# Square sums on VectorE, roots per group on all partitions, rotary keys copied ahead in one hybrid SSD/attention layer

## The chip, the cores and the metric

One core of a Trainium2 chip runs the whole layer. The metric is the device time in microseconds of one execution, from a launch of the program to its end; the median of three runs stands for a kernel. One execution was also recorded by the hardware profiler; its span is the stretch from the first recorded instruction to the last.

## What is computed

One layer of a streaming encoder for 256 prompt frames and 32 sample frames, which share the weights (T = 288 columns), in fp32:

```python
proj = x @ lp['w_in']
gate_pre, z, xbc, dt_raw, q_a, kv_a = jnp.split(proj, IN_SPLITS, axis=-1)
xbc, conv_new = _causal_conv(xbc, conv_state, lp['conv_w'], lp['conv_b'])
...
yh, s_fin = _ssd(xh, dt, a, bm, cm, s0, chunk)
yh = yh + xh * lp['d_skip'].reshape(SSM_GROUPS, HEADS_PER_GROUP, 1)
yg = (yh.reshape(bsz, L, D_INNER) * jax.nn.silu(z)).reshape(bsz, L, SSM_GROUPS, D_INNER // SSM_GROUPS)
yg = _rmsnorm(yg).reshape(bsz, L, D_INNER) * lp['ssm_norm_g']
y_ssm = yg @ lp['w_ssm_proj']
q = ((_rmsnorm(q_a) * lp['q_norm_g']) @ lp['w_q_b']).reshape(bsz, L, MLA_HEADS, QK_NOPE + QK_ROPE)
...
ckv = _rmsnorm(ckv) * lp['kv_norm_g']
kpe = _rope(kpe[:, :, None, :], pos)[:, :, 0, :]
...
mix = (g_ssm * y_ssm + g_mla * y_mla) @ lp['w_out']
h = _layernorm(ALPHA * x + mix, lp['ln1_g'], lp['ln1_b'])
ff = jnp.square(jax.nn.relu(h @ lp['w_up'])) @ lp['w_down']
y = _layernorm(ALPHA * h + ff, lp['ln2_g'], lp['ln2_b'])
```

Three places matter here. `_rmsnorm` is taken over the 512 features of each of two latents (`q_a` and `kv_a`), and over the 256 features of each of the 8 SSD groups. The rotary key `kpe` is 64 features wide.

## The kernel before

Features lie on the 128 partitions and the 288 frames on the free axis, so each activation is a row of blocks of 128x288. A weight chunk is 128x1024 in fp32 (512 KB). SyncE loads the chunks in the order of `chunk_order` into a ring of five slots. For each chunk ScalarE writes a rounded copy `whi` (`hi`, line 908) and VectorE the rest `wlo` (`lo`, line 1300); `ahead(name)` does this for the chunk three places behind the one named. TensorE multiplies in three passes (high by high, high by low, low by high) with operands of type fp32r, in `dense`: 24 matmuls of 288 columns a chunk. Semaphores order the work; every engine runs its own list in the order written.

The stages, in the order of the chunks:

- q0 to q3 and c0 to c3, the two latents. ScalarE squares each block into `qksq` (`latent`), `lat_sums(j)` adds four squared blocks over partitions and blocks by four matmuls with a matrix of ones, ScalarE takes the root, VectorE the reciprocal and the product (`lat_norm`). These ones-matmuls take plain fp32 operands.
- x0 to x31, the conv blocks, the first four ahead of attention and the others among the four attention rounds. `conv_in(b)` on ScalarE takes the block out of PSUM and starts the conv; for that GpSimd has copied three columns of history into `xp` (line 1873, semaphore `xp_state`), and later copies the new history out (line 1875, `xp_saved`). In GpSimd's list conv(0) comes first, then eight copies of the rotated key `krot` onto four quarters of the partitions (`kab`, `kall`, lines 1882 to 1888), four DMAs for the cached keys, and then conv(1).
- The SSD stage, groups 0 to 7. In each, TensorE runs z (two chunks), the gates gs and gm, `outputs`, `states`, and from group 1 on the attention projection m of the group before in two chunks, with small matmuls between: `tokens(g,0..2)`, `cb_products`, `decay_rows(g+1)`. VectorE makes the decay logarithms (`decay_log`), ScalarE their exponentials (`decays`), VectorE `products`, `tokens`, `gated`, `end_state`. `tokens(g,t)` on TensorE writes the bank that VectorE's `tokens` empties (`btok`, line 1546). In group 1 VectorE also splits the attention output (`o_low`, line 1614) for m. `square_sums(g)` adds the squares of two blocks by two ones-matmuls (lines 762 and 763).
- The norm of the groups: `variance` on ScalarE copies a 32-partition slice of the sum into `rstd`; four groups fill the 128 partitions. `roots(h)` then takes one root and `norm_rows(h)` one reciprocal for four groups. `spread(j, bank)` (line 755) puts a group's row back on all partitions by a matmul with a column of the identity. So groups 0 to 3 are normed in iterations 4 to 7 and groups 4 to 7 behind the loop, where `normed`, `norm_high` and `norm_low` write the two parts of `yn`.
- s (the SSD projection, reads `yn`), o, u (32 chunks), d (32 chunks), and the last layernorm.

ScalarE works with function tables; where a new function is not in the loaded set, the list has an ACT_TABLE_LOAD before it.

Of the kernel before, what the change touches and what calls it, by code (L numbers as in the profile page):

```python
# [5 lines left out]
F32 = mybir.dt.float32  # L6
F32R = mybir.dt.float32r
ALU = mybir.AluOpType
# [138 lines left out]
def yn_slot(j):  # L147

    return XB + 4 * (j // 8) + j % 4 + 8 * ((j % 8) // 4)


def layer_program(nc, wst, xT, misc, vecs, consts, ukT, cacheT, cacheK, kpeT, stateS, stateC,
                  o_y, o_ckv, o_kpe, o_ssm, o_conv):
    ctx = ExitStack()
    with ctx:
# [169 lines left out]
        def sems(*names):  # L325
# [27 lines left out]
        s_done, s_ready, sq_done, ss_done, var_in, std_done, rstd_done, bc_done = sems(  # L353
            "s_done", "s_ready", "sq_done", "ss_done", "var_in", "std_done", "rstd_done", "bc_done")
        norm_t, norm_h, norm_lo = sems("norm_t", "norm_h", "norm_lo")
# [68 lines left out]
        def _(pe):  # L424
# [35 lines left out]
            def lat_sums(j):  # L460
                pe.wait_ge(lat_sq, RB * j + RB)
                for k in range(RB):
                    mm = pe.matmul(ps_att[j][:, 0:T], ones, qksq[:, RB * j + k, :], start=k == 0, stop=k == RB - 1)
                mm.then_inc(lat_sum, 1)
# [287 lines left out]
            def spread(j, bank):  # L752

                pe.wait_ge(rstd_done, j // 4 + 1)
                pe.matmul(bank[:, 0:T], ident[:, 32 * (j % 4):32 * (j % 4) + 1].to_broadcast([P, P]),
                          rstd[:, j // 4, :], start=True, stop=True).then_inc(bc_done, 1)

            def square_sums(g):
                pe.wait_ge(sq_done, g + 1)
                if g >= 4:  # L760
                    pe.wait_ge(norm_t, g - 3)
                pe.matmul(ps_ss[:, 0:T], ones, sqs[:, 0, :], start=True, stop=False)
                pe.matmul(ps_ss[:, 0:T], ones, sqs[:, 1, :], start=False, stop=True).then_inc(ss_done, 1)
# [8 lines left out]
            for g in range(GROUPS):  # L772
# [12 lines left out]
                if g >= 4:  # L785
                    pe.wait_ge(var_in, g)
                    spread(g - 4, ps_ss)
# [6 lines left out]
                if g:  # L794
                    dense(("m", g - 1, 1), out, o_rows, 8, False, True)
                    pe.wait_ge(var_in, g)
# [17 lines left out]
            for b in range(4):  # L814
                if b == 0:
                    pe.wait_ge(var_in, GROUPS)
                    pe.wait_ge(s_ready, GROUPS)
                    spread(4, ps_ss)
                    spread(5, ps_s)
                dense(("s", b, 0), ps_att[b], yn_rows, 0, True, False)  # L820
                if b == 1:
                    pe.wait_ge(norm_t, 5)
                    spread(6, ps_ss)
                    pe.wait_ge(norm_t, 6)
                    spread(7, ps_s)
# [1287 lines left out]
```

## Time and profile before

| | us |
|---|---|
| Median of three runs | 857.95 (857.86 to 858.18) |
| The profiled execution | 857.47 |
| Its span | 855.7 |
| TensorE matmul busy | 828.9 (97%) |
| VectorE busy | 568.5 (66%) |
| ScalarE busy | 471.3 (55%) |
| GpSimd busy | 79.7 (9%) |
| Conv blocks 0 to 3 and the way to attention | about 41 to 60 |
| SSD stage | about 336 to 557 |

In the profile PE is TensorE, DVE VectorE, ACT ScalarE and POOL GpSimd. A row of a timeline gives the start and the length of an instruction or of several merged ones (x8 is eight records), and in brackets how long its engine had been idle and what it waited for. Records of matmuls overlap, since they are pipelined: the share of the path that one takes is the step from one start to the next.

### The profile page before, as it was taken

To read this page: it belongs to the slowest core of one execution; us is meant where nothing else is said; L and a number is where in the kernel's file an instruction comes from. 1 tells how busy PE (TensorE), PEld (TensorE's weight loads), DVE (VectorE), ACT (ScalarE), POOL (GpSimd) and SP (SyncE) were. 2 spreads that over 40 slices of the span, in tenths; PEclk is the share of its full clock that TensorE was granted. 3 is DMA by queue.
4 is the path that set the end of the run, shared out by engine and by line. 5 is a ranking of instruction groups with operands and counts; after the bars stand their busy time and mean duration, and the time that the engine had idled before them with its cause. 6 is when DMAs were issued, how large, how long until landed. Compare 5 with 4: busy or idle time off the path is not lost.

```text
span 855.7 us, 15623 instructions
## 1 busy us (share of the span) xinstructions
PE 828.9 (97%) x6359; PEld 787.1 (92%) x6359; DVE 568.5 (66%) x947; ACT 471.3 (55%) x817; POOL 79.7 (9%) x144
## 2 busy tenths in 40 slices
PE   6989999999999999999999999999999999999994
PEld 5988999999899899889998999999999999999994
DVE  5676756655565664886759677676679788755554
ACT  5674546466565466655464455444456888733432
POOL 0053002011011011100000000000000000001112
PEclk9999999999999999999999999999999999999998
DMA  7457325326325423434444353455554545545531
GB/s 289 126 178 291 103 82 176 107 62 196 121 74 173 124 74 116 143 117 124 142 119 140 113 151 114 134 205 165 160 168 149 171 158 164 164 159 172 170 126 56
DMA packets 34183, 123.57 MB, mean 144 GB/s; under 512 B 4224, under 2 KB 4368, under 8 KB 33856
## 3 DMA queue, kind: packets, MB, share of 16 engines
q1 hardware_dynamic: 30816, 110.67, 40.1%
q0 software_dynamic: 3104, 11.24, 3.8%
q8 instruction: 51, 0.84, 0.4%
q10 hardware_dynamic: 192, 0.66, 0.2%
q14 instruction: 20, 0.16, 0.1%
HBM read 118.52 MB, written 4.04 MB: 143 GB/s over the span
## 4 chain that ended last, share of the span: by engine, by line
PE 83%; ACT 6%; DVE 6%; DMA 2%; issue 1%; POOL 1%; ACTq 0%; DVEq 0%; POOLq 0%
PE ps_acc L426 15%; PE ps_acc L428 14%; PE ps_acc L427 14%; PE ps_row L428 3%; PE ps_row L426 3%; PE ps_row L427 3%; PE ps_s L611 3%; PE ps_cb L428 2%; PE ps_tr L428 2%; PE ps_tr L426 2%; PE ps_cb L426 2%; PE ps_tr L427 2%; PE ps_cb L427 2%; ACT prob L1026 2%; DVE wlo L1300 1%; DMA wraw<-in_wst 1%
## 5 line engine op out<-in xcount | busy, mean ns | idle before, releaser
L1300 DVE TENSOR_TENSOR wlo<-wraw,whi 128x1024 fp32r<-128x1024 f32 x204 | 249.4, 1225 | 189.5 <-ACT whi L908 189.1
L908 ACT CAST whi<-wraw 128x1024 fp32r<-128x1024 f32 x204 | 213.2, 1046 | 127.4 <-DMA wraw<-in_wst 126.9
L426 PE MATMUL ps_acc<-xh,whi 128*128 128x288 f32 x576 | 178.2, 309 | 8.3 <-DVE wlo L1300 8.3
L428 PE MATMUL ps_acc<-xh,wlo 128*128 128x288 f32 x576 | 171.0, 297 | 0.0
L427 PE MATMUL ps_acc<-xl,whi 128*128 128x288 f32 x576 | 169.1, 294 | 0.0
L426 PEld LDWEIGHTS ps_acc<-xh,whi 128*128 128x128 f32 x576 | 109.0, 189 | 15.0 <-DVE wlo L1300 8.3
L427 PEld LDWEIGHTS ps_acc<-xl,whi 128*128 128x128 f32 x576 | 110.1, 191 | 0.6
L428 PEld LDWEIGHTS ps_acc<-xh,wlo 128*128 128x128 f32 x576 | 108.8, 189 | 0.0
L1349 DVE SCALAR_TENSOR_TENSOR cv<-xp,vec,cv 128x292 f32<-128x292 f32 x96 | 50.3, 524 | 9.1 <-ACT cv L973 6.7
L426 PE MATMUL ps_acc<-o_h,whi 128*128 128x288 f32 x128 | 39.9, 311 | 0.0
L1875 POOL COPY cnew<-xp 128x6 f32<-128x6 f32 x32 | 15.4, 480 | 241.8 <-ACT xp L970 241.8
L428 PE MATMUL ps_acc<-o_h,wlo 128*128 128x288 f32 x128 | 37.9, 296 | 0.0
L427 PE MATMUL ps_acc<-o_l,whi 128*128 128x288 f32 x128 | 37.4, 293 | 0.0
L426 PE MATMUL ps_acc<-q_h,whi 128*128 128x288 f32 x96 | 29.7, 310 | 3.8 <-ACT xp L970 2.4
L428 PE MATMUL ps_acc<-q_h,wlo 128*128 128x288 f32 x96 | 29.0, 302 | 0.0
L427 PE MATMUL ps_acc<-q_l,whi 128*128 128x288 f32 x96 | 28.6, 298 | 0.0
L428 PE MATMUL ps_row<-e_h,wlo 128*128 128x290 f32 x96 | 28.6, 298 | 0.0
L426 PE MATMUL ps_row<-e_h,whi 128*128 128x290 f32 x96 | 28.6, 297 | 0.0
L427 PE MATMUL ps_row<-e_l,whi 128*128 128x290 f32 x96 | 28.5, 297 | 0.0
L426 PEld LDWEIGHTS ps_acc<-o_h,whi 128*128 128x128 f32 x128 | 24.0, 188 | 1.8 <-issue 0.7
L969 ACT COPY xp<-ps_acc 128x32 f32<-128x32 f32 x32 | 5.9, 183 | 35.2 <-PE ps_acc L428 35.2
L427 PEld LDWEIGHTS ps_acc<-o_l,whi 128*128 128x128 f32 x128 | 24.3, 190 | 0.3
(431 smaller groups left out, 2245.5 us busy)
## 6 DMA issues: line engine op xcount, KB each, us to landing
wraw<-in_wst SPq DMA_DIRECT2D x204, 512.0 KB, 3.5
side<-in_ukT POOLq DMA_DIRECT2D x8, 256.0 KB, 3.8
side_v<-in_ukT POOLq DMA_DIRECT2D x8, 256.0 KB, 3.0
out_ssm<-s_out POOLq DMA_DIRECT2D x8, 256.0 KB, 2.5
x<-in_xT SPq DMA_DIRECT2D x2, 576.0 KB, 4.7
ax<-in_xT POOLq DMA_DIRECT2D x1, 1152.0 KB, 6.0
out_y<-d SPq DMA_DIRECT2D x4, 288.0 KB, 2.1
ckvT<-in_cacheT POOLq DMA_DIRECT2D x1, 1024.0 KB, 7.0
```

The lines of the kernel that those rows point to most:

```text
L426: pe.matmul(out, w, mh, start=first, stop=False)
L427: pe.matmul(out, w, ml, start=False, stop=False)
L428: return pe.matmul(out, wl, mh, start=False, stop=last)
L611: mm = pe.matmul(ps_s[:, c * P:(c + 1) * P], ckvK[0:n, j, c * P:(c + 1) * P], ssT[0:n, j, :], start=j == 0, stop=j == 4)
L908: act.copy(whi[:, s % RING, :], wraw[:, s % RING, :]).then_inc(split_hi, 1)
L969: act.copy(xp[:, u, 264:XW], acc_of(name)[:, SEQ:T])
L1026: e = act.activation(prob[:, h4, a:b], prob[:, h4, a:b], ACT.Exp, bias=stat[:, 1, 4 * q + h4:4 * q + h4 + 1], accum_out=stat[:, 2, 4 * q + ...
L1300: tt(wlo[:, s % RING, :], wraw[:, s % RING, :], whi[:, s % RING, :].bitcast(F32), ALU.subtract).then_inc(split_lo, 1)
L1349: stt(cv[:, u, :], xp[:, u, 1 + tap:1 + tap + CW], v1(V_CONVW + tap * CB + b), cv[:, u, :], ALU.mult, ALU.add).then_inc(tap_chain if tap < ...
L1875: pool.tensor_copy(cnew[:, b, :].rearrange("p (a c) -> p a c", a=2), xp[:, u, 8:XW].rearrange("p (a c) -> p a c", c=36)[:, 6:8, 33:36]).th ...
```

## The change

- `lat_sums(j)`: VectorE adds the four squared blocks in two steps (`lat_squares`, 128x576 and 128x288) and TensorE multiplies once. `lat_squares(0)` stands in VectorE's list after the first half of the rotated key, `lat_squares(1)` before conv(0).
- `square_sums(g)`: VectorE adds the two squared blocks (`square_add`, behind `end_state`) and TensorE multiplies once.
- `spread`, `variance`, `roots` and `norm_rows` go. `root(g)` takes the root of the whole sum on 128 partitions straight from PSUM, one per group, behind `decays(g+1)`; `inverse_root` takes one reciprocal per group. `rstd` keeps two groups. The group g-1 is normed in iteration g, and only the last one behind the loop.
- `yn_slot` puts the low parts of a group over that group's own B and C blocks.
- GpSimd copies the histories of conv blocks 0 and 1 first, then the rotary keys, issues the four DMAs, and then takes conv(0).

```diff
...
 
-    return XB + 4 * (j // 8) + j % 4 + 8 * ((j % 8) // 4)
+    return XB + j // 2 + GROUPS * (j % 2)
 
...
             "tr_done", "tr_free", "xdt_done", "wx_done", "sdec_done", "y_done", "y_free", "yz_done")
-        s_done, s_ready, sq_done, ss_done, var_in, std_done, rstd_done, bc_done = sems(
-            "s_done", "s_ready", "sq_done", "ss_done", "var_in", "std_done", "rstd_done", "bc_done")
-        norm_t, norm_h, norm_lo = sems("norm_t", "norm_h", "norm_lo")
+        s_done, s_ready, sq_done, ss_done, std_done, rstd_done = sems(
+            "s_done", "s_ready", "sq_done", "ss_done", "std_done", "rstd_done")
+        norm_t, norm_h, norm_lo, sq_sum, lat_add = sems("norm_t", "norm_h", "norm_lo", "sq_sum", "lat_add")
         mix_g, mix_t, mix_hi, mix_lo, ax_in, ax_done = sems(
...
             def lat_sums(j):
-                pe.wait_ge(lat_sq, RB * j + RB)
-                for k in range(RB):
-                    mm = pe.matmul(ps_att[j][:, 0:T], ones, qksq[:, RB * j + k, :], start=k == 0, stop=k == RB - 1)
-                mm.then_inc(lat_sum, 1)
+                pe.wait_ge(lat_add, 2 * j + 2)
+                pe.matmul(ps_att[j][:, 0:T], ones, qksq[:, RB * j, :], start=True, stop=True).then_inc(lat_sum, 1)
 
...
 
-            def spread(j, bank):
-
-                pe.wait_ge(rstd_done, j // 4 + 1)
-                pe.matmul(bank[:, 0:T], ident[:, 32 * (j % 4):32 * (j % 4) + 1].to_broadcast([P, P]),
-                          rstd[:, j // 4, :], start=True, stop=True).then_inc(bc_done, 1)
-
             def square_sums(g):
-                pe.wait_ge(sq_done, g + 1)
-                if g >= 4:
-                    pe.wait_ge(norm_t, g - 3)
-                pe.matmul(ps_ss[:, 0:T], ones, sqs[:, 0, :], start=True, stop=False)
-                pe.matmul(ps_ss[:, 0:T], ones, sqs[:, 1, :], start=False, stop=True).then_inc(ss_done, 1)
+                pe.wait_ge(sq_sum, g + 1)
+                if g:
+                    pe.wait_ge(std_done, g)
+                pe.matmul(ps_ss[:, 0:T], ones, sqs[:, 0, :], start=True, stop=True).then_inc(ss_done, 1)
 
...
                 states(g)
-                if g >= 4:
-                    pe.wait_ge(var_in, g)
-                    spread(g - 4, ps_ss)
                 if g:
...
                     dense(("m", g - 1, 1), out, o_rows, 8, False, True)
-                    pe.wait_ge(var_in, g)
                     square_sums(g)
...
             for b in range(4):
-                if b == 0:
-                    pe.wait_ge(var_in, GROUPS)
-                    pe.wait_ge(s_ready, GROUPS)
-                    spread(4, ps_ss)
-                    spread(5, ps_s)
                 dense(("s", b, 0), ps_att[b], yn_rows, 0, True, False)
-                if b == 1:
-                    pe.wait_ge(norm_t, 5)
-                    spread(6, ps_ss)
-                    pe.wait_ge(norm_t, 6)
-                    spread(7, ps_s)
             for b in range(4):
...
                 act.wait_ge(yz_done, g + 1)
+                if g:
+                    act.wait_ge(ss_done, g)
                 act.activation(sqs[:], xc[:, 2 * g:2 * g + 2, 0:T], ACT.Square).then_inc(sq_done, 1)
 
-            def variance(g):
+            def root(g):
                 act.wait_ge(ss_done, g + 1)
-                f = slice(32 * (g % 4), 32 * (g % 4) + 32)
-                act.copy(rstd[f, g // 4, :], ps_ss[f, 0:T]).then_inc(var_in, 1)
-
-            def roots(h):
-                act.wait_ge(var_in, 4 * h + 4)
-                act.activation(rstd[:, h, :], rstd[:, h, :], ACT.Sqrt, scale=1.0 / (2 * P),
+                if g >= 2:
+                    act.wait_ge(norm_t, g - 1)
+                act.activation(rstd[:, g % 2, :], ps_ss[:, 0:T], ACT.Sqrt, scale=1.0 / (2 * P),
                                bias=v1(V_EPS)).then_inc(std_done, 1)
...
                 ahead(("z", 2 * g))
+                decays(g)
                 if g:
-                    variance(g - 1)
-                    if g == 4:
-                        roots(0)
-                decays(g)
+                    root(g - 1)
                 if g == 0:
...
                 squares(g)
-                if g >= 4:
-                    norm_high(g - 4)
+                if g:
+                    norm_high(g - 1)
                 if g:
...
             ahead(("m", GROUPS - 1, 0))
-            variance(GROUPS - 1)
-            roots(1)
+            root(GROUPS - 1)
             ahead(("m", GROUPS - 1, 1))
-            norm_high(4)
             ahead(("s", 0, 0))
-            norm_high(5)
+            norm_high(GROUPS - 1)
             ahead(("s", 1, 0))
-            norm_high(6)
-            norm_high(7)
             ahead(("s", 2, 0))
...
                 dve.wait_ge(m_dve, count[0])
+
+            def lat_squares(j):
+
+                sq = qksq[:, RB * j:RB * j + RB, :]
+                dve.wait_ge(lat_sq, RB * j + RB)
+                tt(sq[:, 0:2, :], sq[:, 0:2, :], sq[:, 2:4, :], ALU.add).then_inc(lat_add, 1)
+                dve.wait_ge(lat_add, 2 * j + 1)
+                tt(sq[:, 0, :], sq[:, 0, :], sq[:, 1, :], ALU.add).then_inc(lat_add, 1)
 
...
             tt(krot[:, 0, :], kt[:, 2, :], kt[:, 3, :], ALU.subtract).then_inc(krot_done, 1)
+            lat_squares(0)
             ahead(("c", 0))
...
                ).then_inc(acum_split, 1)
+            lat_squares(1)
             conv(0)
...
 
-            def norm_rows(h):
-                dve.wait_ge(std_done, h + 1)
-                dve.reciprocal(rstd[:, h, :], rstd[:, h, :]).then_inc(rstd_done, 1)
-
-            def normed(j, bank):
-                dve.wait_ge(bc_done, j + 1)
+            def square_add(g):
+                dve.wait_ge(sq_done, g + 1)
+                tt(sqs[:, 0, :], sqs[:, 0, :], sqs[:, 1, :], ALU.add).then_inc(sq_sum, 1)
+
+            def inverse_root(g):
+                dve.wait_ge(std_done, g + 1)
+                dve.reciprocal(rstd[:, g % 2, :], rstd[:, g % 2, :]).then_inc(rstd_done, 1)
+
+            def normed(j):
+                dve.wait_ge(rstd_done, j + 1)
                 if j:
...
                 for q in range(2):
-                    y = stt(yt[:, q, :], xc[:, 2 * j + q, 0:T], v1(V_SSMG + 2 * j + q), bank[:, 0:T],
+                    y = stt(yt[:, q, :], xc[:, 2 * j + q, 0:T], v1(V_SSMG + 2 * j + q), rstd[:, j % 2, :],
                             ALU.mult, ALU.mult)
...
                 dve.wait_ge(norm_h, j + 1)
-                tt(yn[:, yn_slot(2 * j):yn_slot(2 * j) + 2, 0:T], yt[:], yn[:, 2 * j:2 * j + 2, 0:T].bitcast(F32),
+                tt(yn[:, yn_slot(2 * j):yn_slot(2 * j + 1) + 1:GROUPS, 0:T], yt[:], yn[:, 2 * j:2 * j + 2, 0:T].bitcast(F32),
                    ALU.subtract).then_inc(norm_lo, 1)
...
                     o_low(2)
-                elif g == 4:
-                    norm_rows(0)
+                if g:
+                    inverse_root(g - 1)
                 ahead(("gm", g))
...
                 end_state(g)
+                square_add(g)
                 if g:
                     ahead(("m", g - 1, 0))
-                if g >= 4:
-                    normed(g - 4, ps_ss)
+                if g:
+                    normed(g - 1)
                 if g + 1 < GROUPS:
...
                     ahead(("m", g - 1, 1))
-                if g >= 4:
-                    norm_low(g - 4)
+                if g:
+                    norm_low(g - 1)
 
...
             mla_gated(GROUPS - 2)
-            norm_rows(1)
+            inverse_root(GROUPS - 1)
             ahead(("m", GROUPS - 1, 1))
-            normed(4, ps_ss)
-            norm_low(4)
-            normed(5, ps_s)
+            normed(GROUPS - 1)
             ahead(("s", 0, 0))
-            norm_low(5)
+            norm_low(GROUPS - 1)
             mla_gated(GROUPS - 1)
             ahead(("s", 1, 0))
-            normed(6, ps_ss)
-            norm_low(6)
-            normed(7, ps_s)
-            norm_low(7)
             ahead(("s", 2, 0))
...
         def _(pool):
-            def conv(b):
-
-                u, name = b % 2, ("x", b)
-                if b == 0:
-                    pool.wait_ge(cst_in, 16)
-                    pool.wait_ge(xp_zero, 1)
+            def history(b):
+
                 if b >= 2:
                     pool.wait_ge(conv_done, b - 1)
-                pool.tensor_copy(xp[:, u, 261:264], cstate[:, b, :]).then_inc(xp_state, 1)
+                pool.tensor_copy(xp[:, b % 2, 261:264], cstate[:, b, :]).then_inc(xp_state, 1)
+
+            def conv(b):
+
+                u, name = b % 2, ("x", b)
+                if b >= 2:
+                    history(b)
                 wait_evac(pool, name)
...
 
-            conv(0)
+            pool.wait_ge(cst_in, 16)
+            pool.wait_ge(xp_zero, 1)
+            history(0)
+            history(1)
             pool.wait_ge(krot_done, 2)
-            pool.wait_ge(xp_saved, 1)
             for q in range(4):
...
                                ).then_inc(kall_in, 16)
-            for b in range(1, X_FIRST):
+            for b in range(X_FIRST):
                 conv(b)
...
```

## Rows read from the trace of the kernel before

**Rows 1.** The page: span and its first part, busy time of each engine.

```profile
span 855.7 us, 15623 instructions
...
PE 828.9 (97%) x6359; PEld 787.1 (92%) x6359; DVE 568.5 (66%) x947; ACT 471.3 (55%) x817; POOL 79.7 (9%) x144
```

**Rows 2.** Waits of PE over the span: total us, times, longest us.

```profile
PE ps_acc L426 <- ACT xp L970: 2.4, 1, 2.4
PE ps_tr L701 <- DVE btok L1546: 1.7, 3, 0.6
PE ps_acc L426 <- ACT qn L1010: 1.2, 1, 1.2
```

**Rows 3.** Timeline of PE: start us, length us, then the instruction.

```profile
44.33 2.10 PE L463 MATMUL ps_row<-qksq,con 128*128 128x288 f32 x8
...
46.40 0.29 PE L427 MATMUL ps_acc<-xl,whi 128*128 128x288 f32 x1
```

**Rows 4.** Timeline of PE at the start of attention.

```profile
59.73 0.58 PE L426 MATMUL ps_acc<-q_h,whi 128*128 128x288 f32 x1 [2.44 <-ACT xp L970]
60.10 0.44 PE L427 MATMUL ps_acc<-q_l,whi 128*128 128x288 f32 x1
...
69.46 0.37 PE L426 MATMUL ps_acc<-q_h,whi 128*128 128x288 f32 x1 [1.25 <-ACT qn L1010]
```

**Rows 5.** Windows: us, busy by engine, granted clock, DMA share, GB/s.

```profile
60.00:63.00 3.00, 3.00 (x13) 2.79 (x13) 2.78 (x4) 2.20 (x6) 1.43 (x2) 0.51 0.04 14
```

**Rows 6.** Timeline of ACT, 31 to 56 us.

```profile
31.88 1.28 ACT L934 ACT_TABLE_LOAD   x1 [0.34 <-PE ps_row L463]
...
35.01 0.41 ACT L928 ACTIVATE qksq<-ps_acc 128x288 f32<-128x288 f32 x1 [1.33 <-PE ps_acc L428]
...
54.85 0.63 ACT L973 ACTIVATE cv<-xp,vec 128x292 f32<-128x292 f32 x1 [3.99 <-POOL xp L1873]
```

**Rows 7.** Groups of instructions over the span: busy us, mean ns, idle before.

```profile
L1300 DVE TENSOR_TENSOR wlo<-wraw,whi 128x1024 fp32r<-128x1024 f32 x204 | 249.4, 1225 | 189.5 <-ACT whi L908 189.1
...
L1123 ACT ACT_TABLE_LOAD x7 | 9.0, 1283 | 0.1
...
L1608 DVE TENSOR_TENSOR yn<-yt,yn 128x576 fp32r<-128x576 f32 x8 | 6.0, 750 | 2.2 <-ACT yn L1146 2.2
...
L1595 DVE RECIPROCAL rstd<-rstd 128x288 f32<-128x288 f32 x2 | 3.9, 1943 | 0.7 <-ACT rstd L1141 0.7
```

**Rows 8.** Timeline of DVE, 40 to 47 us.

```profile
40.86 0.45 DVE L1381 SCALAR_TENSOR_TENSOR dt_v<-dt_r,dt_a 32x288 f32<-32x288 f32 x1 [2.22 <-ACT dt_a L955]
...
46.30 0.45 DVE L1393 TENSOR_TENSOR acum_s<-acum,acum_s 32x288 fp32r<-32x288 f32 x1
```

**Rows 9.** Timeline of ACT in group 4: the old root.

```profile
440.66 1.28 ACT L1141 ACT_TABLE_LOAD   x1
441.95 0.54 ACT L1141 ACTIVATE rstd<-rstd,vec 128x288 f32<-128x288 f32 x1
```

**Rows 10.** Timeline of PE in groups 1 and 6.

```profile
369.92 0.50 PE L701 MATMUL ps_tr<-con,xc 128*32 128x128 f32 x3 [0.54 <-DVE btok L1546]
...
377.52 0.40 PE L426 MATMUL ps_acc<-o_h,whi 128*128 128x288 f32 x1
...
507.17 0.49 PE L701 MATMUL ps_tr<-con,xc 128*32 128x128 f32 x3
```

**Rows 11.** Timeline of DVE in groups 1, 6 and 7.

```profile
376.12 1.34 DVE L1614 TENSOR_TENSOR o_l<-o,o_h 128x1152 fp32r<-128x1152 f32 x1
...
504.54 0.28 DVE L1546 COPY btok<-ps_tr 128x128 f32<-128x128 f32 x1
...
513.13 0.48 DVE L1576 SCALAR_TENSOR_TENSOR ysb<-xc,vec,ps_row 128x256 f32<-128x256 f32 x1 [3.02 <-PE ps_row L739]
...
519.39 2.16 DVE L1527 SCALAR_TENSOR_TENSOR seg<-ps_row,tokv,con 128x128 f32<-128x128 f32 x8 [1.63 <-PE ps_tr L691]
...
540.70 0.48 DVE L1576 SCALAR_TENSOR_TENSOR ysb<-xc,vec,ps_row 128x256 f32<-128x256 f32 x1 [3.02 <-PE ps_row L739]
```

More of the change, by code:

```diff
@@ L1864, in _ @@
         def _(pool):
+            def history(b):
+                if b >= 2:
+                    pool.wait_ge(conv_done, b - 1)
+                pool.tensor_copy(xp[:, b % 2, 261:264], cstate[:, b, :]).then_inc(xp_state, 1)
             def conv(b):
                 u, name = b % 2, ("x", b)
-                if b == 0:
-                    pool.wait_ge(cst_in, 16)
-                    pool.wait_ge(xp_zero, 1)
                 if b >= 2:
-                    pool.wait_ge(conv_done, b - 1)
-                pool.tensor_copy(xp[:, u, 261:264], cstate[:, b, :]).then_inc(xp_state, 1)
+                    history(b)
                 wait_evac(pool, name)
```

## The prediction

> **What bounds the kernel now.** I first read the busy times of the page: TensorE (PE) is busy 828.9 of 855.7 us, 97% [rows 1]. The reader should see that hardly any other engine's work can count by itself: what shortens the kernel is either an instruction taken off PE or a wait of PE. The profiled execution took 857.47 us, 0.48 under the median 857.95. I make the sum as a difference and take it off the median.
>
> Next the waits of PE. Apart from the start and small ones they are few [rows 2]: 2.4 us on ScalarE (ACT) once, 1.2 us on ACT once, 1.7 us in three waits for `btok` on VectorE (DVE). The first is followed by slow matmuls. After the wait the records stand 0.24 us apart instead of 0.13 [rows 3, 4], and in 60 to 63 us the granted clock is 0.51 with DMA nearly idle [rows 5], which is the 1.2 GHz level. 13 matmuls by 0.11 us are 1.4 us. The two waits of 2.4 and 1.2 stand at 59.73 and 69.46 [rows 4]. Behind them lies the row of ACT at 54.85, which waited 3.99 us for GpSimd (POOL): POOL was copying rotary keys before it fetched the history of conv block 1 [rows 6].
>
> **What leaves PE.** The latent sums go from 4 matmuls to 1, twice (6 removed), the group sums from 2 to 1, eight times (8), and the 8 spreads go. Each plain fp32 matmul is recorded twice (x8 for four) [rows 3]. Its price is its share of the path, not the length of a record, since records overlap: four take from 44.33 to one dense step (0.13) before 46.40, 1.94 us, thus 0.485 each [rows 3]. 22 by 0.485 is 10.7 us: 2.9 in the latents, 7.8 in the SSD stage (3.9 sums, 3.9 spreads). PE is bound on both sides of each, so all of this counts unless a wait takes its place. That is the question.
>
> **The latent stage.** The sum now waits for two adds of DVE. For the first latent they stand right after the first rotary subtract and end some microsecond before PE asks; nothing is lost and 1.46 us is won. For the second, PE asks at 44.33 minus 1.46, 42.9. But the adds stand in DVE's queue behind the second split of `acum`, recorded at 46.30 for 0.45 us [rows 3, 8]. How much earlier can DVE be there? It idled 2.22 us until ACT's logarithm at 40.86 [rows 8]. ACT's chain to it starts at c1's square at 35.01, which waited 1.33 us for PE [rows 6]. PE will be 1.46 earlier, ACT's root before it 0.34 earlier [rows 6], so ACT runs on from 33.4, 1.6 earlier, and so does DVE: it reaches the adds at 45.15. The wide one takes 0.75 (the 128x576 subtract of line 1608, 750 ns [rows 7]), the other some 0.45 (half the columns; between 0.38 and 0.75). They end at 46.35, so PE newly stands still for **3.5 us** (bounds: 2.2 if all of DVE's idle were recovered and the adds ran at their least, 5.0 if none is).
>
> For what a stop does to the clock the nearest row is the one at 59.73: 2.44 us idle after small transposes, and 1.4 us lost at the 1.2 GHz level [rows 4, 5]; the stop of 1.25 us at 69.46 left it alone. I take 1.4 here too (bounds 0 and 2). Queued behind the adds on DVE is conv(0), and behind PE's wait all of conv blocks 1 to 3.
>
> **The moved copies.** POOL now copies both histories first, then makes the eight key copies from about 31 us and issues the four loads of `kall`, then takes conv(0). ACT's wait of 3.99 us goes, as its history lies ready. ACT's conv_in(1) then hangs on PE's own x1. Following ACT (root at 48.8, table, `wend` by 51, x1 at 51.3, then the silu table and two splits) x2's bank is free at 56.7, and PE reaches the attention stage at 59.3: no wait. It then runs at full clock, so 2.44 + 1.4 us return, and the wait of 1.25 at 69.46 falls too, as conv(1) to conv(3) on DVE are about 3 us earlier (0 to 0.6 of it may stay). The four DMAs and the later `ckvT` work of POOL are earlier as well; PE waits for none of them now. The copies run beside DVE's splits at 32 to 38 us, where DVE has the 2.22 us idle [rows 8]: nothing.
> Sum to 69.46: 2.9 - 3.5 - 1.4 + 2.4 + 1.4 + 1.2 = **3.0 us gained** (1.0 to 4.5).
>
> **The SSD stage, group 1.** ACT gains per group a root: one more table (1.283, as each line-1123 load [rows 7]) and a 0.54 Sqrt [rows 9], 1.82, in place of a copy of 0.39; it lies between `decays` and `z_block`, ahead of the split that lets DVE go on to `products`, `tokens(g,1)` and so PE's `tokens(g,2)`. In group 1 before, PE already waited there: 0.54 us, start 369.92 [rows 10]. DVE's new add shifts the decay rows by 0.6, the copy's wait for PE is gone, the root comes: 1.2 us later in all. With PE 0.35 ahead, its start goes from 0.35 early to 1.2 late: 1.55 lost. Then DVE meets `inverse_root(0)`, 1.943 us [rows 7], ahead of `o_low(3)`. That split was recorded at 376.12 for 1.34, ending 377.46, and PE's first `m` chunk, which waits for it, started at 377.52, just in time [rows 10, 11]. So it now starts 1.2 + 1.9 = 3.1 us late; another **1.9 lost**. Behind `inverse_root` are queued the split of gm+3, `o_low(3)`, `gated` and the whole decay log of group 2, which ends some 4 us later. In group 2 that costs another 0.4 at the tokens wait.
>
> **Groups 3 to 7.** Here I look at slack. In group 6 DVE had released the tokens bank at 504.82 and PE asked at 507.17: 2.35 us [rows 10, 11]. The root takes 1.82 of it, a moved or vanished variance copy returns 0 to 0.6, a later decay log takes up to 0.6: 0 to 0.2 us wait, I take 0.1. The 1.94 us reciprocal goes before `gated`, where DVE idled 3.02 us; the add goes before the decay log, where it idled 1.63 [rows 11]. Groups 6 and 7 stand 27.57 apart (513.13 and 540.70 [rows 11]); less one sum and one spread, PE's new group is 26.6. Against it I set one turn of the work that must follow in order: from the end of a decay log ACT's split and decays 2.8, root 1.8, silu table and `z_block` 1.7, the next split on ACT and on DVE 2.2, products and second tokens 3.2, split and third tokens 2.3, `s_dec` and reciprocal 2.4, split 1.2, gate and end of state 2.7, the add 0.5, split 1.2, norm 0.9, decay log 3.3: 26.2. It just fits, and what it has over is 0.4. Group 4's old wait of 0.60 (the old root stood before the decays) falls to 0.1. The four spreads of the tail save 1.9, and its one remaining norm has 12 us before the second half of `s` needs it.
> Sum: 7.8 - 0.1 - 1.55 - 1.9 - 0.4 - 0.1 + 0.5 - 0.3 = **3.9 us gained** (bounds: 8.9 with no new wait and the old ones of 0.54 and 0.60 gone; 1.5 lost at 0.9 more per group over six).
>
> **A rule weighed.** A table load took 1.28 us from 440.66, and the Sqrt behind it started at 441.95, 0.01 after its end [rows 9]. The Trainium skill, "ScalarE: Activation LUTs", section "What ACT_TABLE_LOAD costs", puts a drain of some 1.38 us on top of each switch. By that rule the turn round the engines would be about 1 us too long per group and the time some 857.
>
> **Rivals.** (A) *The group-1 delays are absorbed.* If DVE and ACT catch up before PE asks, only the early stall stays: 3.0 + 8.9, time 846.0. For it: DVE is idle a quarter of this stage. Against: PE already waited at 369.92, and 377.52 follows the split by 0.06. (B) *The ring of DVE and ACT becomes the bound.* Place: decay log, decays, root, z_block, split, products, reciprocal, gate. It decides once it exceeds PE's 26.6 us per group; from 1.15 us over, in six groups, all 6.9 us are gone. At 1.5 over: 860.1. For it: the slack of 0.4 is small and hangs on late weights. Against: the old waits in rows 11 that would be used up first. (C) *The early stall is longer*, 5.0 us or repeated at conv_in(1), so the stage returns 0: 854.0. (D) *The copies do not help*: ACT would wait again at conv_in(1), 3.7 us of 6.9 gone, 854.8. The order of POOL's queue speaks against it. (E) *A switch of tables costs more than its row.* If something as long as a second load (1.283 [rows 7]) lay behind each new one, the ring would be 27.5, 0.9 over; six groups lose 5.4: 856.5. Against it: the Sqrt behind a load starts 0.01 us after its end [rows 9]. The drain of the Trainium skill's page above would be such a cost.
>
> **How the numbers follow.** 3.0 + 3.9 = 6.9, so 857.95 - 6.9 = **851.1 us**. Chances: forecast 0.56, A 0.17, B 0.12, C 0.09, D 0.04, E 0.02. The range 845.5 to 856.5 takes in A, C and D and the forecast's own bounds, and leaves out B and the far end of A; E lies on its edge. A measurement tells about 0.2% (1.7 us) from no change. B splits into 0.04 same and 0.08 slower, E is same, and so are 0.02 of the forecast and of C each: faster 0.82, same 0.10, slower 0.08.
>
> **What would show it.** Right: in the waits of PE a new one of 3 to 4 us at the latent matmul near 43, released by DVE's add, slow clock behind it; no wait at the start of the attention stage and full clock there; group 1's tokens and first `m` matmul each some 2 us idle; `rstd` roots once per group with two more table loads around; groups 4 to 7 about 26.6 us apart against 27.57. Wrong: no idle at 43 (the adds come earlier than I place them), or waits over 0.5 us in each later group.

## Result and the profile of the changed kernel

The changed kernel takes 853.45 us (median of four, 852.8 to 853.63) against 857.9 us of the kernel before (857.69 to 858.18): ratio 0.9943, 95% interval 0.9931 to 0.9955. It is faster by 4.5 us by the medians, 4.9 by the ratio; forecast were 6.9 us, 851.1. Gains below are differences of medians. The profiled execution took 852.8 us, 4.7 less than that of before, close enough to compare the two profiles as they are.

The page of the changed kernel, its parts that answer to [rows 1]:

```profile
span 851.0 us, 15560 instructions
...
PE 820.7 (96%) x6315; PEld 781.2 (92%) x6315; DVE 584.2 (69%) x965; ACT 477.5 (56%) x820; POOL 79.4 (9%) x144
```

The 44 records that are gone are the 22 plain matmuls, each recorded twice. The waits of PE (engine, line waited for: total us, times, longest), which answer to [rows 2]; the wait at the start of the span, ahead of them, and those under 1 us are left out:

```profile
PE ps_row L462 <- DVE qksq L1303: 3.6, 1, 3.6
PE ps_tr L699 <- DVE btok L1526: 1.9, 2, 1.3
PE ps_acc L426 <- DVE o_l L1598: 1.8, 1, 1.8
PE ps_acc L426 <- ACT qn L987: 1.1, 1, 1.1
```

The 2.4 us wait on `xp` is gone, the 1.2 on `qn` is still there, and two new ones have come: 3.6 on the latent add and 1.8 on `o_l`. The same four in PE's timeline, with the matmuls that say how the clock was; they answer to [rows 3, 4, 10]:

```profile
46.45 1.33 PE L462 MATMUL ps_row<-qksq,con 128*128 128x288 f32 x2 [3.59 <-DVE qksq L1303]
...
47.82 0.45 PE L427 MATMUL ps_acc<-xl,whi 128*128 128x288 f32 x1
48.06 0.45 PE L428 MATMUL ps_acc<-xh,wlo 128*128 128x288 f32 x1
...
59.34 0.24 PE L486 MATMUL ps_tr<-con,dt_v 32*128 32x32 f32 x1
...
60.50 0.38 PE L426 MATMUL ps_acc<-q_h,whi 128*128 128x288 f32 x1
...
68.22 0.37 PE L426 MATMUL ps_acc<-q_h,whi 128*128 128x288 f32 x1 [1.13 <-ACT qn L987]
...
370.04 0.50 PE L699 MATMUL ps_tr<-con,xc 128*32 128x128 f32 x3 [1.34 <-DVE btok L1526]
...
379.45 0.40 PE L426 MATMUL ps_acc<-o_h,whi 128*128 128x288 f32 x1 [1.80 <-DVE o_l L1598]
```

Behind the first stop matmuls stand 0.24 us apart. In the windows (us, busy by engine, granted clock, DMA share, GB/s) the clock is 0.50 there, the 1.2 GHz level, and again behind the last stop:

```profile
48.00:50.00 2.00, 2.00 (x11) 2.00 (x10) 1.39 (x2) 1.97 (x3) 0.00 (x0) 0.50 0.02 4
...
380.00:384.00 4.00, 4.00 (x21) 4.00 (x20) 3.88 (x9) 0.68 (x1) 0.72 (x1) 0.57 0.13 45
```

What it cost follows from distances. From the latent matmul to the first `dt_v` transpose it is 12.9 us here (46.45 to 59.34). In the kernel before it is 11.55 with the x8 group of [rows 3] (44.33, and the first row of the next fence), less three plain matmuls of 0.485: 10.1. So 2.8 us of PE's way were lost at the lower clock. In group 1 the first `m` chunk starts 1.9 us later than in the kernel before (377.52 [rows 10]) and the next one 3.5 us later: 1.5 us.

The `dt_v` row of the kernel before:

```profile
55.88 0.24 PE L488 MATMUL ps_tr<-con,dt_v 32*128 32x32 f32 x1
```

DVE, around the two stops, answering to [rows 8, 11]:

```profile
44.67 0.45 DVE L1372 TENSOR_TENSOR acum_s<-acum,acum_s 32x288 fp32r<-32x288 f32 x1
45.15 0.76 DVE L1301 TENSOR_TENSOR qksq<-qksq 128x576 f32<-128x576 f32 x1
45.94 0.46 DVE L1303 TENSOR_TENSOR qksq<-qksq 128x288 f32<-128x288 f32 x1
...
375.12 1.93 DVE L1579 RECIPROCAL rstd<-rstd 128x288 f32<-128x288 f32 x1
...
378.06 1.33 DVE L1598 TENSOR_TENSOR o_l<-o,o_h 128x1152 fp32r<-128x1152 f32 x1
```

The adds start in the order of the queue, behind the split of `acum`; the reciprocal stands ahead of the last split of `o`, for which PE waits.

### The profile page after: what moved, and what is told of

It is laid out like the page before. It is cut to its first block, busy times and chain, and to the rows that moved or that the text cites. A ratio compares the mean times of both kernels' runs of the same rounds, so it can differ in the third digit from the quotient of the medians.

```text
span 851.0 us, 15560 instructions
## 1 busy us (share of the span) xinstructions
PE 820.7 (96%) x6315; PEld 781.2 (92%) x6315; DVE 584.2 (69%) x965; ACT 477.5 (56%) x820; POOL 79.4 (9%) x144
## 4 chain that ended last, share of the span: by engine, by line
PE 82%; DVE 8%; ACT 6%; DMA 2%; issue 1%; ACTq 0%; DVEq 0%
PE ps_acc L426 15%; PE ps_acc L428 15%; PE ps_acc L427 14%; PE ps_row L428 3%; PE ps_row L426 3%; PE ps_row L427 3%; PE ps_s L609 3%; DVE wlo L1270 2%; PE ps_tr L428 2%; PE ps_cb L428 2%; PE ps_tr L426 2%; PE ps_cb L426 2%; PE ps_cb L427 2%; PE ps_tr L427 2%; ACT prob L1003 2%; DMA wraw<-in_wst 1%
```

## The experiments

The expectations give times against the kernel before, which was timed with each kernel on the same chip (858.36, 858.87 and 858.36 us in the three sets). The first three kernels take the change apart.

**Only the copies.** The kernel before, with GpSimd's program of the changed one.

```diff
-            conv(0)
+            pool.wait_ge(cst_in, 16)
+            pool.wait_ge(xp_zero, 1)
+            history(0)
+            history(1)
             pool.wait_ge(krot_done, 2)
-            pool.wait_ge(xp_saved, 1)
...
-            for b in range(1, X_FIRST):
+            for b in range(X_FIRST):
                 conv(b)
```

> The kernel before with the GpSimd part of the change alone. Theory: TensorE's stop of 2.4 us at 59.73, the slow clock behind it (1.4 us) and most of the stop of 1.25 us at 69.46 go, since ScalarE no longer waits 4.0 us for the history of conv block 1: 4.0 us less, about 853.9, full clock from 57 us on. Rival: the wait of ScalarE turns into another one of the same length (conv on VectorE, the weights): within 1 us of the kernel before.

Measured: 854.36 us, ratio 0.9954 (0.9942 to 0.9967), 4.0 us gained. In PE's timeline the two waits of [rows 4] became

```profile
59.96 0.40 PE L426 MATMUL ps_acc<-q_h,whi 128*128 128x288 f32 x1 [0.52 <-ACT xp L970]
...
66.62 0.37 PE L426 MATMUL ps_acc<-q_h,whi 128*128 128x288 f32 x1 [1.25 <-ACT qn L1010]
```

at full clock. Four microseconds come from the order of a queue whose engine is busy 9% of the span: the 3.99 us for which ACT waited [rows 6] had come out at PE as a stop and a slow stretch. The profile is of the slowest of the five executions (855.34) and shows less of it: ACT starts the conv of block 1 at 51.99 instead of 54.85, and PE leaves its second wait 2.8 us earlier. That wait stayed at 1.25, though the blocks came earlier.

**Only the latent sums.**

```diff
-                pe.wait_ge(lat_sq, RB * j + RB)
-                for k in range(RB):
-                    mm = pe.matmul(ps_att[j][:, 0:T], ones, qksq[:, RB * j + k, :], start=k == 0, stop=k == RB - 1)
-                mm.then_inc(lat_sum, 1)
+                pe.wait_ge(m_dve, 5 * j + 5)
+                pe.matmul(ps_att[j][:, 0:T], ones, qksq[:, RB * j, :], start=True, stop=True).then_inc(lat_sum, 1)
...
+            lat_squares(1)
             conv(0)
```

> The kernel before with the latent sums on VectorE alone; the copies stay where they were. Theory: TensorE stops 3.6 us at 43 us and runs slowly for some 6 us behind it, and under this stop GpSimd's copies are done before ScalarE needs the history, so the stage ends where it ends with both edits: 1.2 us less than before, about 856.7. Rival: the two edits add up, and as the copies alone are worth 4 us, the latent sums alone cost 2.8 us: about 860.7.

Measured: 857.61 us, 0.9989 (0.998 to 0.9998), 0.8 gained, the smallest gain here, with an interval that nearly touches no change. The rival's 860.7 fell. PE's stop at the sum was 3.88 us and the clock fell behind it (0.57 in 46 to 50 us). And the stop at the start of attention was gone without any change on GpSimd: ACT met conv block 1 at 54.00 and waited for PE, not for GpSimd.

```profile
47.25 1.32 PE L462 MATMUL ps_row<-qksq,con 128*128 128x288 f32 x2 [3.88 <-DVE qksq L1330]
```

This is the main finding on the early stage. Each of the two parts removes the same old stop with its slow stretch, and they can't both be paid for it: apart they gain 4.0 and 0.8, together they leave PE 1.1 us ahead from 82 us on by the first profile of the changed kernel (1.5 by the second, below). With the latent sums in place, the copies bring little.

**Only the SSD part.** The changed kernel with latent sums and GpSimd's program put back.

```diff
-                pe.wait_ge(lat_add, 2 * j + 2)
-                pe.matmul(ps_att[j][:, 0:T], ones, qksq[:, RB * j, :], start=True, stop=True).then_inc(lat_sum, 1)
+                pe.wait_ge(lat_sq, RB * j + RB)
+                for k in range(RB):
+                    mm = pe.matmul(ps_att[j][:, 0:T], ones, qksq[:, RB * j + k, :], start=k == 0, stop=k == RB - 1)
...
-            history(0)
-            history(1)
+            conv(0)
```

> The changed kernel with the latent sums and the GpSimd part put back as before, so that only the SSD stage is changed. Theory: the stage's own balance in the two traces, 3.6 us less than before: about 854.3, with the stops of 1.3 and 1.8 us in group 1 and the slow clock behind them. Rival: the stops in group 1 come from the earlier start of TensorE and are smaller here: about 852.5.

Measured: 855.69 us, 0.9965 (0.9952 to 0.9978): 2.7 gained by the medians, 3.0 by the ratio (1.9 to 4.1). The stops of group 1 were the same, 1.33 and 1.79, and the clock fell behind the second. In the profile PE reaches 85.12 where it was at 83.53 in the kernel before, although nothing is changed up to there: 1.0 us was lost at the start of the span, and the slow stretch behind the old stop of 2.44 was longer (granted clock 0.50 from 62 to 68 us). Behind that point 3.3 us are gained, near the 3.6 expected; the rival's smaller stops did not come.

**The adds earlier.** The changed kernel, the adds of latent 1 ahead of `lat_low(0)`; they then stand before DVE's idle time.

```diff
+            lat_squares(1)
             lat_low(0)
             ...
-            lat_squares(1)
             conv(0)
```

> The changed kernel with the two adds for the second latent moved ahead in VectorE's list, before the split of the query latent. Theory: the stop of 3.6 us shrinks to about 0.4 us and the clock stays full behind it, but ScalarE's list (root, exponentials, conv in and out) then sets the start of attention, so new waits of 1 to 2 us stand at the query chunks, and 2.3 us come back: about 851.2. Rival A: all of the stop and of the slow clock come back, 6.5 us: about 847.0. Rival B: nothing comes back because ScalarE was the bound all along: 853.5.

Measured: 850.78 us, 0.991 (0.9897 to 0.9924), 7.6 gained: 3.1 more than the change did at first, 2.0 more than when it was measured again (5.5, last experiment). The stop shrank to 0.38:

```profile
44.34 0.75 PE L462 MATMUL ps_row<-qksq,con 128*128 128x288 f32 x2 [0.38 <-DVE qksq L1303]
...
59.12 0.40 PE L426 MATMUL ps_acc<-q_h,whi 128*128 128x288 f32 x1 [1.26 <-ACT xp L947]
```

The time is near the 851.2 expected; both rivals, 847.0 and 853.5, fell. The clock stayed at 1.00 from 42 to 72 us. So the place of the adds in DVE's queue was the cause of the stop. Not all of the 6.0 us (3.2 of the stop, 2.8 of the clock) is kept: behind the wait for `qn` PE is 2.45 us ahead of where the changed kernel has it (65.77 against 68.22), or some 3.5 if one allows for a first dense stretch that ran 1.1 us longer in this profile. The late PE of the changed kernel had covered the wait of 1.26 for `xp`; this and smaller gaps behind it took the rest. Again one stop hid another. ACT no longer waits for PE here: from 45.80, where it had waited 0.67 for weights, its list runs on without a wait to the conv of block 1 at 51.16. Of the whole difference of the two profiles, 3.1 us, another part is no work of the edit: in group 1 the stop of 1.80 is there unchanged, but this time the clock stayed up behind it.

**The stop filled.** The changed kernel with six plain matmuls on constants ahead of the latent sum, so that PE works through most of the stop; their results are not used.

```diff
+                if j:
+                    pe.wait_ge(dt_pre, 1)
+                    for k in range(6):
+                        pe.matmul(ps_ss[:, 0:T], ones, cos, start=True, stop=True)
                 pe.wait_ge(lat_add, 2 * j + 2)
```

> The changed kernel with six matmuls of constants (2.9 us, results unused) put into TensorE's stop ahead of the second latent sum. Theory: the slow clock behind the stop comes from the idle stretch, so with 0.7 us idle instead of 3.6 the granted clock stays 1.00 in the 6 us behind; conv block 1 ends 2.8 us earlier, of which ScalarE's list lets 1.3 us through: about 1.3 us less than the changed kernel, 5.8 less than before. Rival: the clock falls there for another reason (the two latent matmuls, the pause of the loads): slow records stay and the time is that of the changed kernel or longer.

Measured: 851.59 us, 0.9917 (0.9902 to 0.9931), 7.3 gained. The sum starts at the same point, 46.4, for it still awaits the adds, but at full clock:

```profile
46.42 0.75 PE L466 MATMUL ps_row<-qksq,con 128*128 128x288 f32 x2 [0.68 <-DVE qksq L1307]
...
56.62 0.24 PE L490 MATMUL ps_tr<-con,dt_v 32*128 32x32 f32 x1
```

10.2 us to the transposes instead of 12.9; the five profiles with the stop of 3.6 to 3.9 us left open took 11.5 to 13.0. So the slow stretch came from the idle time of PE, and behind the wait for `qn` PE is 2.05 us ahead of the changed kernel (66.17 against 68.22), by work without use. In the times the gain is 1.9 us over the changed kernel's first median (853.45) and 1.2 over its second (852.81, last experiment), measured in other sets; the intervals of the ratios overlap with that of the second, so the trace shows the gain better than the times. Part of it may be group 1, where the clock stayed up in this profile behind a stop of 1.79.

**Both stops of group 1 filled.**

```diff
+                if g == 1:
+                    pe.wait_ge(std_done, 1)
+                    pe.matmul(ps_ss[:, 0:T], ones, cos, start=True, stop=True)
+                    pe.matmul(ps_ss[:, 0:T], ones, cos, start=True, stop=True)
                 tokens(g, 2)
...
+                if g == 1:
+                    for k in range(3):
+                        pe.matmul(ps_ss[:, 0:T], ones, cos, start=True, stop=True)
                 if g:
                     pe.wait_ge(o_lo, ROUNDS)
```

> The changed kernel with constant matmuls (results unused) put into the two stops of group 1: two ahead of tokens(1,2) and three ahead of the first m chunk. Theory: idle stretches shrink from 1.3 and 1.8 us to about 0.3 each, the granted clock stays 1.00 in 380 to 384 us, and 1.5 us come back: about 6 less than before. Rival: the clock falls all the same and the time is that of the changed kernel (4.5 less than before).

Measured: 851.37 us, 0.9917 (0.9903 to 0.9931), 7.5 gained; clock 1.00 from 366 to 388 us. Here too the matmuls' results are unused. The two stops of 1.34 and 1.80 became one of 0.37, and the tokens and the `m` chunk stand where they did, since DVE's data come no earlier. What the clock gained can't be told from this run alone, for the changed kernel itself did not always lose it there (last experiment), and behind the untouched latent stop only 1.3 us were lost here instead of 2.8.

**Group 0's root and reciprocal late.** In group 1 ACT takes the root behind the gate, and DVE the reciprocal behind the split of the `m` chunk; the last split of `o` is then no longer behind it.

```diff
-                if g:
+                if g > 1:
                     root(g - 1)
...
                 gate(("gm", g), tm[:, g % 2, :], KB + g)
...
+                elif g == 1:
+                    root(0)
...
-                if g:
+                if g > 1:
                     inverse_root(g - 1)
...
                     ahead(("m", g - 1, 0))
+                if g == 1:
+                    inverse_root(0)
```

> The changed kernel, in group 1 alone the root of group 0 is taken behind the gate gm on ScalarE, and its reciprocal behind the split of m(0,0) on VectorE, ahead of the norm. Theory: the stop of 1.3 us at the tokens falls back to the old 0.5, the stop of 1.8 us at the first m chunk goes, and with it the slow clock there (1.5 us): about 4.4 us less than the changed kernel, 9 less than the kernel before. Rival A: the reciprocal of 1.9 us now delays the decay log of group 2 and TensorE stops in group 2 instead: 6 to 7 us less than before. Rival B: the slow clock at 380 us has nothing to do with the stops and stays: 7.5 us less than before.

Measured: 850.7 us, 0.9907 (0.9891 to 0.9923), 8.2 gained, between the 9 of the theory and the 6 to 7 of rival A. Both stops of group 1 are gone (the 0.56 that is left for the tokens stands in group 0, as before), so their cause is shown: the root ahead of the split on ACT, and the reciprocal ahead of `o_low(3)` on DVE. The latent stop is still 3.60, but with 1.6 us of slow clock, not 2.8; that part of the 8.2 is not the edit's. Now the decay log of group 2 and, behind it, `mla_gated(0)`, which frees the bank of z block 5, come late:

```profile
390.04 0.40 PE L426 MATMUL ps_acc<-xh,whi 128*128 128x288 f32 x1 [1.91 <-DVE mixm L1605]
```

**Both moves.** The edits of the last and of "the adds earlier" together.

```diff
+            lat_squares(1)
             lat_low(0)
...
+                elif g == 1:
+                    root(0)
...
+                if g == 1:
+                    inverse_root(0)
```

> The two moves together: adds of the second latent early, root and reciprocal of group 0 late. Theory: the two places are independent, so their gains add up: the changed kernel is 4.5 us under the kernel before, the early adds gave 3 more and the late root gives 4.4 more, about 12 us less than before (some 846.3). Rival: a gain in one place is waited away in the other (weights or VectorE as the next bound): not more than 9 us less.

Measured: 849.37 us, 0.989 (0.9875 to 0.9905), 9.5 gained, not 12: nearer to the rival, which allowed 9. PE stops again 1.91 for `mixm`, this time with a slow stretch behind it (1.4 us), and waits 1.25 for `xp` and 1.25 for `qn` ahead of the attention rounds. Against the 4.5 to 5.5 of the changed kernel the moves alone had brought some 2 to 3.7 us each; together they bring 4 to 5, as the new waits come in.

**Group 0's scaling moved into group 2.** The last kernel, with DVE's reciprocal and scaling behind the first token piece of group 2, its low part behind the second, and ACT's high part behind the first z block.

```diff
+                if g == 2:
+                    norm_high(0)
...
                 tokens(g, 0)
                 ending(g, 0)
+                if g == 2:
+                    inverse_root(0)
+                    normed(0)
...
+                if g == 2:
+                    norm_low(0)
...
-                if g == 1:
-                    inverse_root(0)
-                if g:
+                if g > 1:
                     normed(g - 1)
```

> Both moves as in the kernel with the latent adds early and group 0's root late (849.37 us), and besides group 0's reciprocal and scaling (1.94 + 0.95 us of VectorE) and its low part (0.74) leave group 1: VectorE does them in group 2 behind mla_gated(0) and the first token piece, and ScalarE's high part moves behind the first z block. Theory: the 1.91 us stop of PE on mixm in group 2, and the 1.4 us of slow clock behind it, came from mla_gated(0) being queued behind these 3.6 us on VectorE; both go: 846.1 us, 12.8 below the kernel before on a chip where that has 858.9. VectorE idled 2.22 us in group 2 where the reciprocal now stands, so it should delay nothing. Rival 1: the 2.9 us make the high and low parts of the weights of z block 5 late and PE stops there by 0.7 to 1.5 us instead: 847 to 848. Rival 2: the stop on mixm isn't due to this queue (it waits for m(0,0)'s end on PE itself): no change, 849.4.

Measured: 847.81 us, 0.9873 (0.9858 to 0.9887), the fastest kernel here, 5.0 us under the changed one in the same set. The wait for `mixm` is gone, but

```profile
394.54 0.50 PE L699 MATMUL ps_tr<-con,xc 128*32 128x128 f32 x3 [1.69 <-DVE btok L1530]
```

stands in its place: ACT's high part (its row below) waited for DVE's scaling and held up the split of z block 5, and so `products` and the token bank. Rival 1 had the cause, a late split for z block 5, but PE met it one step on, at the tokens. Rival 2 fell. The gain over the last kernel, 1.6 us by the medians of two sets, is the size of the slow stretch, which did not follow this stop; stops of this length have it only sometimes (last section).

```profile
389.01 0.68 ACT L1122 CAST yn<-yt 128x576 fp32r<-128x576 f32 x1 [1.93 <-DVE yt L1590]
```

**The changed kernel once more,** without an edit.

> The changed kernel once more, unaltered. Theory: the slow clock behind a stop of 1.8 us (group 1, o_l) isn't fixed by the kernel but varies from execution to execution, since kernels with the same stop showed it (changed kernel, SSD part alone) or didn't (adds early, stop at 43 us filled). Then this profile may have no slow stretch at 378 to 384 us and a time up to 1.5 us lower. Rival: it depends on what the kernel does ahead of the stop, so it is there again, 1.5 us of it. The 3.59 us stop at 46 us has its slow clock, 2.9 us, by both. Time 853.4 by the rival, 852 to 853.4 by the theory.

Measured: 852.81 us, 0.9935 (0.9918 to 0.9952), 5.5 gained. Its stops are those of the first profile, 3.60, 1.35 and 1.80, yet

```profile
380.00:384.00 4.00, 4.00 (x30) 3.76 (x29) 3.87 (x8) 0.69 (x1) 1.43 (x3) 1.00 0.27 67
```

the clock stays up behind the 1.80, and behind the 3.60 only 1.5 us are lost (11.7 us from 47.09 to the transpose below, against 10.2). What a stop costs at the clock is not fixed by the kernel. The four executions took 851.74, 851.88, 853.73 and 854.05, with mean granted clocks of 0.993, 0.993, 0.991 and 0.991: the longer ones spent more of their time at the lower level.

```profile
47.09 1.33 PE L462 MATMUL ps_row<-qksq,con 128*128 128x288 f32 x2 [3.60 <-DVE qksq L1303]
...
58.77 0.24 PE L486 MATMUL ps_tr<-con,dt_v 32*128 32x32 f32 x1
```

## Why the prediction was right, and by how much it missed

**The sign and most of the mechanism held; the size was 2.2 us too large in the profile:** 4.7 (855.7 to 851.0) instead of 6.9.

**What leaves PE.** Groups 2 and 3 are 0.49 us shorter each, groups 5 to 7 0.97: one sum, then one sum and one spread at 0.485. In [rows 11] the gates of groups 6 and 7 stood 27.57 apart; now

```profile
512.39 0.48 DVE L1556 SCALAR_TENSOR_TENSOR ysb<-xc,vec,ps_row 128x256 f32<-128x256 f32 x1 [1.18 <-PE ps_row L737]
...
539.00 0.48 DVE L1556 SCALAR_TENSOR_TENSOR ysb<-xc,vec,ps_row 128x256 f32<-128x256 f32 x1 [1.22 <-PE ps_row L737]
```

26.61, forecast 26.6. The tail gave 1.9, as forecast.

**The latent stage.** The stop came where it was put, 3.59 against 3.5, and the adds began at 45.15 to the hundredth. The step that failed is the price of the clock, taken from another stop: 1.4 where 2.8 were lost (1.5 in the second profile). The gain at the old stop, on the other side, had been priced too low. At the `dt_v` transposes PE is 3.5 us later than in the kernel before (59.34 against 55.88), at the second wait 1.2 us earlier (68.22 against 69.46 [rows 4]). Less the 0.1 by which that wait shrank, 4.6 us came back, where 2.4 + 1.4 stood in the sum. The slow records themselves cost 1.6 (14 steps take 3.50 us from 59.73, 1.94 from 60.50 in the changed kernel); the rest is small gaps beside the stop and at 64.80.

**The wait at 69.46** was to fall with the stop before it (0 to 0.6 left). It stayed, 1.13 now, and 1.24 to 1.25 in the kernels with the copies alone, the adds early and the stop filled. What PE waits for there is the end of a chain of ACT and DVE that begins at the conv of block 1:

```profile
53.10 0.19 ACT L946 COPY xp<-ps_acc 128x32 f32<-128x32 f32 x1 [1.32 <-PE ps_acc L428]
...
53.60 0.63 ACT L950 ACTIVATE cv<-xp,vec 128x292 f32<-128x292 f32 x1
```

In the kernel before this conv starts at 54.85, when GpSimd's history has come [rows 6], and 14.61 us later PE goes on. Here it starts at 53.60, when PE's x1 has come, and 14.62 later PE goes on. In all eleven profiles in which PE waits for `qn` the distance is 14.61 to 14.63; only in that of the SSD part alone is PE the later one. So up to this point the early stage gained what the conv of block 1 gained, 1.25 us. The stop at 59.73 and the slow stretch behind it did not lengthen the stage: without them PE would, by these distances, have waited longer for `qn`. The prediction paid for the stop, the stretch and the wait one by one, with convs "about 3 us earlier". Along the chain its miss is one term: it had PE's x1 at 51.3, and it came at 53.10. Of these 1.8 us, 1.4 are the clock priced too low. Added along PE, the early sum of 3.0 came to 2.9 - 3.6 - 2.8 + 4.6 + 0.1 = 1.2. That such a sum was off by no more than 1.8 is in part luck, for it held both a wait that did not fall (1.2 too much) and a return at the old stop that was 0.8 too small.

**Group 1.** The token wait grew to 1.34: PE lost 1.4, forecast 1.55. The reciprocal ahead of `o_low(3)` delayed the `m` chunk by 1.8, forecast 1.9. The cause is shown by the kernel with the late root, where both go. Not foreseen: 1.5 us of slow clock behind this 1.80 us stop. The sum had the mechanism at hand and applied it to the early stop alone; in the second profile nothing was lost there.

**The later groups.** 0.8 us of small waits were forecast for groups 2 to 7, and none came: the old one of 0.60 in group 4 went too. In group 6 DVE now releases the bank at 505.60 and PE asks at 506.44: the slack is 0.84 of the former 2.35. So 1.5 of it went, near the 1.8 that the forecast gave to the root, and what was over sufficed.

```profile
505.33 0.27 DVE L1526 COPY btok<-ps_tr 128x128 f32<-128x128 f32 x1
...
506.44 0.49 PE L699 MATMUL ps_tr<-con,xc 128*32 128x128 f32 x3
```

The SSD stage gained 3.6, forecast 3.9; by parts it is 7.8 - 1.4 - 1.8 - 1.5 + 0.6 = 3.7. That it came so near is luck in part: 1.5 us of slow clock that the sum did not have took the place of waits that it had.

**The table rule.** The new root in group 4:

```profile
443.82 1.28 ACT L1117 ACT_TABLE_LOAD   x1
445.11 0.50 ACT L1117 ACTIVATE rstd<-ps_ss,vec 128x288 f32<-128x288 f32 x1
445.63 1.28 ACT L1100 ACT_TABLE_LOAD   x1
446.93 0.41 ACT L1100 ACTIVATE zt<-ps_acc 128x288 f32<-128x288 f32 x1
```

Each instruction starts 0.01 to 0.02 us behind the end of the load. The drain of 1.38 us of the Trainium skill, "ScalarE: Activation LUTs", "What ACT_TABLE_LOAD costs", is not in this trace, and rival E with it; PE has no wait over 0.3 us in groups 3 to 7, so neither did the ring of DVE and ACT become the bound (B). Rival A fell: both waits of group 1 came as priced. C, at 854.0, came nearest to the time: the early stage did cost more than forecast, but by the clock behind the stop, not by a longer stop. D did not happen: ACT waited for PE at conv block 1, not for GpSimd.

## What to carry to other kernels

Two edits that each remove the wait ahead of a stage are paid for it once: before you add them up, run the sum with one done and ask which stop is left for the other. Waits and slow stretches of one stage don't add up if they all lie under one chain on other engines: take the last wait of the stage, follow it back to where its chain begins (here 14.6 us earlier, at the conv of block 1), and count only what moves that point. And where an operation is moved onto an idle engine, look at what stands behind it in that engine's queue: here 1.2 us of adds and 1.9 us of reciprocal, both on a DVE that is idle for 31% of the span, made up 9.7 us of standing and slow clock on PE in the first profile (3.6 + 2.8 + 1.8 + 1.5). Moving the adds ahead of other work, and group 0's root with its scaling a group later, gave 5.0 us.

## What was unexpected of the hardware

What followed a stop of PE, in the profiles of this case:

| stop, us | kernel | lost at the lower clock, us |
|---|---|---|
| 3.88 | latent sums only | 2.8 |
| 3.59, 3.60 | changed, twice | 2.8; 1.5 |
| 3.60, 3.59 | late root; both stops of group 1 filled | 1.6; 1.3 |
| 2.44 | before; SSD part only | 1.6; some 2.5 |
| 1.91 | late root; both moves | 0; 1.4 |
| 1.80 | changed, twice | 1.5; 0 |
| 1.80, 1.79 | adds early; stop at 43 us filled | 0; 0 |
| 1.79 | SSD part only | 1.5 |
| 1.69 | scaling in group 2 | 0 |
| 1.24 to 1.26 | before, and five others, ahead of the attention rounds | 0 |

Every stop of 2.4 us or more in these traces was followed by a stretch at the 1.2 GHz level, none of 1.36 or less was, and of those of 1.7 to 1.9 some were: the same kernel with the same stop showed it once and once not. What decides between them was not settled. For a forecast this means that a stop of 1.7 to 1.9 us is priced with 0 to 1.5 us besides its length, and one of 3.6 with 1.3 to 2.8.

The start of the span varies too. Behind PE's first wait (8.2 to 8.5 us) the first matmuls stand 0.24 us apart, the distance of the lower level, though the clock column shows 1.00 there; 11 such steps were recorded for the changed kernel and 12 for the kernel before, but 21 with the adds early and 23 with the SSD part alone. At 0.11 us a step, two profiles can so differ by 1.3 us ahead of any edit.
